# A two-block transformer kernel: tile 0 of the last stage put in order sooner, and its row buffers joined later

## The chip, the cores and the metric

The kernel runs on one core of a Trainium2 chip. A core has five engines with their own instruction queues (TensorE or PE, VectorE or DVE, ScalarE or ACT, GpSimd or POOL, SyncE or SP), which meet only through semaphores, a working memory (SBUF) of 128 partitions, and an accumulator memory (PSUM) of eight banks of 512 floats per partition. Data come from the chip's main memory by DMA. The metric is the time of one execution in microseconds (us); lower is better.

## The reference

One sequence of 256 tokens of width 1024 passes two layers of a first block (gated linear attention beside a state-space mixer, then a dense and an eight-expert feed-forward) and one layer of a second block. The change touches the second block alone:

```python
def token_mixer(h, p, attend):
    z = h @ p['w_in'] + p['b_in']                 # 1024 -> 5120 columns
    q = rmsnorm_2(z[..., COL_Q:COL_K] ...); k = rmsnorm_2(z[..., COL_K:COL_V] ...)
    v = z[..., COL_V:COL_G_HY] ...
    y_hy = hyena(z[..., COL_HY:COL_Q], p) @ p['w_hy_out']     # two long convolutions
    y_na = attend(q, k, v).reshape(B, L, D_NA) @ p['w_na_out']
    gate = jax.nn.sigmoid(z[..., COL_G_HY:N_PROJ])
    merged = gate[..., :D_MODEL] * y_hy + gate[..., D_MODEL:] * y_na
    return merged @ p['w_out']

def peer(h, p):
    q = (hf @ p['peer_w_q']).reshape(T, PEER_HEADS, 2, PEER_D_HALF)     # 8 heads, 2 halves
    s = jnp.einsum('thpd,hpnd->thpn', q, p['peer_keys'])                # 128 keys a half
    top_s, top_i = lax.top_k(s, PEER_TOPK)                              # 16 of each half
    cand_s = top_s[:, :, 0, :, None] + top_s[:, :, 1, None, :]          # 256 sums
    best_s, best_pos = lax.top_k(cand_s, PEER_TOPK)                     # 16 experts
    idx = ...; g = jax.nn.softmax(best_s, axis=-1)
    act = gelu(einsum('td,thkd->thk', xb, u_tab[idx]))                  # 1024 floats a row
    return einsum('thk,thkd->td', g * act, v_tab[idx])                  # 1024 floats a row
...
x_next = x + g1 * token_mixer(modulate(x, ...), p)
x_next = x_next + g2 * peer(modulate(x_next, ...), p)
```

Each token needs 8 x 16 experts, and each expert is one row of 2048 floats (u and v side by side, 8 KB) out of 16384.

## The kernel before, in words

Every engine runs one function, written in the order in which it executes. Where engines meet, the code waits for a semaphore's count. The 256 tokens are two tiles of 128. The work around the change is in three parts.

**The hyena part** (PE L1235 to L1256). Two convolutions `o`, each: turn the input (`ytm`), a transform (`yre`, `yim`), a product on VectorE (`spectrum`), the inverse (`conv`, L684, 128x256 matmuls), and VectorE's update. PE fills its waits with `fill`, which takes the next `piece` of the input projection. A piece (L762) multiplies 256 columns of `w_in`, held in a ring of five 2 MB slots. After it comes the normalising of q, k and kc (L1262 to L1291): PE sums squares (L1269), ScalarE takes the root, VectorE the reciprocal, PE spreads it (L1280), VectorE applies it, PE permutes for the rotary embedding. Between them VectorE works off `hidden`: products of the modulation weights `w_ada` (L1545, four a tile of weights). The gate columns' projections (3072 and 3584, two pieces each) fill PE here. When a slot's last reader is done, SP loads the next weights into it, in its fixed order: `w_hy` into the slot of 3072, then 4096 into that of 3584, then `w_ada`.

**The sixteen head turns** (PE L1366 to L1400; eight heads of tile 0, then eight of tile 1 in `head_turns`, each turn being one head for 128 tokens with i = 0 to 15 and `t` the tile). One turn: VectorE adds the bias and finds the peak (L2037 to L2041), ScalarE exponentiates, VectorE scales (L2047), PE turns the weights (L692) and multiplies by v (L684), in the PSUM banks 4 and 5. Two places in each turn are filled: with `first` (the products of `y_hy` and the last gate pieces) while t = 0, then with `na0` (y_na's product), `out0` (`w_out`, L1340) for tile 0, whose attention is complete after turn 7. Then follow tile 0's residual (`added`), squares, their sum (L1354), a root, a spread (L1361), `normed` and ScalarE's shift, after which tile 0 can ask for experts: `query` (L1422), `key_scores` (L1435), and on VectorE `choices`.

**The row stage** (256 rows, i // 128 the tile, i % 128 = 16 x head + place). POOL issues an indirect DMA for each row: 128 experts, one a partition, 1 MB. VectorE takes the dot product with the tokens (L2199), ScalarE gelu, VectorE multiplies by the gate (L2178), ScalarE makes a diagonal, and PE accumulates 8 matmuls (L1473). Between rows VectorE makes the `choices` of the head after next, PE the remaining queries. `row_places` says which of 16 buffers each row uses. Eight exist at the start; the others are memory that query weights still hold, and join in pairs:

```python
    joins = {50: (8, 9), 82: (10, 11), 98: (12, 13), 116: (14, 15)}
    for i in range(256):
        turn.extendleft(joins.get(i, ()))
        b = turn.popleft()
        turn.append(b)
        ...
                lambda: (at(0), P["pq", 5]),
                lambda: (at(14618), P["pq", 7]),
                lambda: (part(("w_pq", 0), 0), P["pq", 9]),
                lambda: (part(("w_pq", 1), 0), P["pq", 11])
```

Before the first use of such a buffer POOL waits (L2703) for the query that was its last reader: jobs 5, 7, 9 and 11, whose last parts stand in PE's program ahead of rows 44, 76, 93 and 111 (`job_rows`). Any other buffer is free when PE is done with the row it held. POOL's queue is in order: what stands behind a waiting row waits as well.

## Time and profile before

| | us |
|---|---|
| median of 3 runs | 2723.76 (2721.18 to 2724.1) |
| the profiled execution | 2724.18 |
| its span, first to last instruction | 2721.7 |
| PE busy in it | 2522.6 |
| VectorE busy | 2074.8 |
| ScalarE busy | 1256.5 |
| POOL busy | 265.9 |
| bytes moved | 824.92 MB, mean 303 GB/s |

The profile's page gives busy times, a line of 40 slices of 68 us, and the chain of work that ended last. The second block takes roughly the time from 1640 us, the head turns 1877 to 1998, the rows 2020 to 2717. All times below are from the span's start.

### The profile page before, as it was taken

What the parts mean: (1) busy time and instruction counts of PE and PEld (TensorE: products, weight loads), DVE (VectorE), ACT (ScalarE), POOL (GpSimd) and SP (SyncE); (2) the same over time, 40 slices, a digit from 0 to 9 for tenths busy, and PEclk for the clock granted to TensorE, in tenths of its full rate; (3) what the DMA queues carried; (4) which work ended last, traced back from release to release, by engine and by line L of the source; (5) the groups of instructions that cost most, each with busy time, mean ns of one, the idle gap of its engine ahead of it and who ended that gap; (6) DMA issues with size and microseconds to landing.
All of it is one profiled execution on the core that took longest, in us unless ns stands there. A gap on an engine that the chain in (4) does not pass through costs nothing. (4 is left out here: it accounts for less than half of the span.)

```text
span 2721.7 us, 38026 instructions
## 1 busy us (share of the span) xinstructions
PE 2522.6 (93%) x14586; PEld 2183.4 (80%) x14586; DVE 2074.8 (76%) x3114; ACT 1256.5 (46%) x1544; POOL 265.9 (10%) x286
## 2 busy tenths in 40 slices
PE   5999999999999999999999989988988998888787
PEld 4789997787888888888888877647887987787786
DVE  6778984767898989889998964535758785698875
ACT  3234443236777777777777753102323332233322
POOL 0000001000000000000000000000013333343331
PEclk9989999989999999999999998999989999899899
DMA  8647774547999999999999945304749998899997
GB/s 344 248 173 291 277 287 180 230 180 296 355 355 356 356 339 349 356 357 355 354 355 353 356 170 211 124 31 163 286 157 357 391 421 335 368 419 421 420 420 325
DMA packets 109562, 824.92 MB, mean 303 GB/s; under 512 B 11896, under 2 KB 15224, under 8 KB 16128
## 3 DMA queue, kind: packets, MB, share of 16 engines
q1 hardware_dynamic: 71792, 551.75, 53.3%
q0 software_dynamic: 36864, 268.45, 24.1%
q8 instruction: 117, 1.92, 0.3%
q10 hardware_dynamic: 720, 2.24, 0.2%
q14 instruction: 69, 0.57, 0.1%
HBM read 821.34 MB, written 1.05 MB: 302 GB/s over the span
## 5 line engine op out<-in xcount | busy, mean ns | idle before, releaser
L1811 DVE TENSOR_TENSOR ring_r<-ring,arena_r 128x2048 fp32r<-128x2048 f32 x336 | 770.1, 2292 | 11.5
L2225 ACT ACTIVATE arena_r<-ring 128x2048 fp32r<-128x2048 f32 x378 | 725.7, 1920 | 28.9 <-DMA ring<-in_ffn_w_down 12.8
L698 PE MATMUL ps<-arena_r 128*128 128x512 f32 (+1 forms) x1120 | 417.2, 373 | 1.5 <-DVE arena_r L1847 1.5
L700 PE MATMUL ps<-arena_r 128*128 128x512 f32 x896 | 349.3, 390 | 0.0
L699 PE MATMUL ps<-ring_r,arena_r 128*128 128x512 f32 x896 | 348.6, 389 | 0.0
L1473 PE MATMUL ps<-sel,ring 128*128 128x128 f32 x2240 | 291.3, 287 | 58.4 <-ACT sel L2225 45.5
L1473 PEld LDWEIGHTS ps<-sel,ring 128*128 128x128 f32 x2240 | 274.3, 200 | 73.9 <-ACT sel L2225 58.2
L2225 ACT ACTIVATE sel<-cs,arena 128x128 f32<-128x128 f32 x256 | 102.8, 402 | 402.4 <-DVE arena L2178 374.5
L1473 PE MATMUL ps<-sel,arena 128*128 128x128 f32 x1856 | 235.0, 287 | 43.1 <-ACT sel L2225 41.7
L1473 PEld LDWEIGHTS ps<-sel,arena 128*128 128x128 f32 x1856 | 224.8, 201 | 50.5 <-ACT sel L2225 48.5
L2225 ACT ACTIVATE arena<-ps 128x512 f32<-128x512 f32 (+2 forms) x208 | 103.4, 497 | 328.4 <-PE ps L684 94.5
L698 PEld LDWEIGHTS ps<-arena_r 128*128 128x128 f32 x1120 | 211.3, 189 | 35.6 <-DVE arena_r L1847 1.8
L2199 DVE CUSTOM_DVE_ANT_0 accb<-ring,ps 128x1024 f32<-128x1024 f32 x140 | 171.0, 1221 | 52.9 <-DMA ring<-in_uv,arena 49.8
L700 PEld LDWEIGHTS ps<-arena_r 128*128 128x128 f32 x896 | 168.2, 188 | 35.7
L699 PEld LDWEIGHTS ps<-ring_r,arena_r 128*128 128x128 f32 x896 | 168.4, 188 | 34.2
L2704 POOL DMA_INDIRECT ring<-in_uv,arena x140 | 131.9, 942 | 624.8 <-DVE arena L2059 368.0
L699 PE MATMUL ps<-arena_r 128*128 128x256 f32 x672 | 192.5, 286 | 0.0
L698 PE MATMUL ps<-arena_r,h_r 128*128 128x512 f32 x448 | 178.4, 398 | 3.0 <-DVE ring_r L1811 1.7
L700 PE MATMUL ps<-arena_r,h_r 128*128 128x512 f32 x448 | 175.2, 391 | 0.0
L699 PE MATMUL ps<-ring_r,h_r 128*128 128x512 f32 x448 | 174.8, 390 | 0.0
L2225 ACT ACTIVATE arena<-arena 128x1 f32<-128x1 f32 (+5 forms) x361 | 112.6, 312 | 107.8 <-DVE arena L2004 17.3
L2199 DVE CUSTOM_DVE_ANT_0 accb<-arena,ps 128x1024 f32<-128x1024 f32 x116 | 141.6, 1221 | 25.2 <-DMA arena<-in_uv,arena 21.3
(285 smaller groups left out, 3894.3 us busy)
## 6 DMA issues: line engine op xcount, KB each, us to landing
ring<-in_moe_w_gate SPq DMA_DIRECT2D x112, 1024.0 KB, 5.0
ring<-in_moe_w_up SPq DMA_DIRECT2D x112, 1024.0 KB, 5.2
ring<-in_moe_w_down SPq DMA_DIRECT2D x112, 1024.0 KB, 4.9
ring<-in_ada_w SPq DMA_DIRECT2D x24, 1024.0 KB, 9.8
ring<-in_ada_w SPq DMA_DIRECT2D x12, 2048.0 KB, 7.9
ring<-in_w_in SPq DMA_DIRECT2D x10, 2048.0 KB, 12.1
ring<-in_w_ada SPq DMA_DIRECT2D x8, 2048.0 KB, 8.2
ring<-in_ffn_w_gate SPq DMA_DIRECT2D x14, 1024.0 KB, 5.1
```

Of the source, the lines that this page charges most:

```text
L698: e.matmul(out, xs[0], ws[0], start=start, stop=False, skip_group_check=True)
L699: e.matmul(out, xs[0], ws[1], start=False, stop=False, skip_group_check=True)
L700: return e.matmul(out, xs[1], ws[0], start=False, stop=stop, skip_group_check=True)
L1473: last = e.matmul(ps.banks[2 * t + c // 4][:, 128 * (c % 4):128 * (c % 4) + 128], rows[:, 1024 + 128 * c:1152 + 128 * c], m.diag[:, i % ND ...
L1811: v(e.tensor_tensor(ring_low[ring.half[unit]], ring.buf[unit], mo.high[unit_at[unit] % NHIGH].bitcast(F32), ALU.subtract), ("low", unit))
L2199: v(e.tensor_tensor_reduce(m.waste, row_buffer(i)[0][:, 0:1024], x, 1.0, 0.0, ALU.mult, ALU.add, m.dots[:, i:i + 1]), ("dots", i))
L2225: A.mark(e.activation(out, src, func, **kw), name)
L2704: e.indirect_dma_start(base, None, T["uv"], bass.IndirectOffsetOnAxis(m.index[t][:, n:n + 1], 0)).then_inc(row_sems[ROWS[i][0]], 16)
```

## The change

Five edits.

1. `joins` moves from rows 50, 82, 98, 116 to 54, 88, 106, 126.
2. The two pieces of projection 3072 are cut into four halves: two inside the second convolution, two behind it. Their results stay in PSUM banks 0 and 1 (`HELD`), since their place in SBUF is still occupied by the filters, and the second convolution rotates over banks 2 to 7 (`REST`). 3584 takes the fills of q and k; kc has two halves of the `y_hy` product.
3. VectorE does four `hidden` products ahead of the first peak and fewer in the turns; merging moves up one turn.
4. In the turns of tile 1 `na0`, `out0`, the squares, root, spread, norm and shift move one or two turns earlier, and the first query is asked in turn 15.
5. Tile 0's head 0: the best 8 of each half give 64 sums, whose best 8 are the first 8 experts; the second best 8 and all 256 sums follow behind. Squares and sum of tile 1 move two rows up, `exp_gates` of head 1 stands beside the root at row 8 (it was row 8, the root row 7), query job 2 is asked one row sooner, and from the second head on `choices` skips each fourth row.

```diff
-    joins = {50: (8, 9), 82: (10, 11), 98: (12, 13), 116: (14, 15)}
+    joins = {54: (8, 9), 88: (10, 11), 106: (12, 13), 126: (14, 15)}
...
+            gates = chain.from_iterable(piece(3072, i, 2, hT, "hT x", HELD) for i in range(2))
             for o in range(2):
+                among = REST if o else range(8)
...
+                if o:
+                    next(gates)
                 for k in range(2):
...
                 fill(1)
+                if o:
+                    next(gates)
                 e.wait_ge(*V["spectrum", o, 1])
...
             P.at["hyena done"] = P.now
+            next(gates)
+            next(gates)
...
-            pieces = [piece(c0, i, 2, hT, "hT x") for c0 in (3072, 3584) for i in range(2)]
+            pieces = [piece(3584, i, 2, hT, "hT x") for i in range(2)]
...
+                if x == "kc":
+                    next(first)
                 fill(1)
...
-            fill(1)
+            next(first)
...
                 if t == 0:
                     some(first, 1)
-                elif i < 10:
-                    some(na0, 1)
-                elif i < 12:
+                elif i == 8:
+                    some(na0, 2)
+                elif i < 11:
                     some(out0, 2)
+                elif i == 13:
+                    peer_spread(0)
                 elif i == 15:
-                    peer_spread(0)
+                    query(0, 0)
...
-                elif i == 12:
+                elif i == 11:
                     peer_sums(0)
+                elif i == 15:
+                    query(0, 1)
...
+            some(hidden, 4)
             peak(0)
...
                 if i < 8:
-                    some(hidden, 3)
+                    some(hidden, 3 if 3 <= i < 7 else 2)
...
-                if i == 14:
+                if i == 12:
                     rstd(("norm_peer", 0), pr.scr[:, 2048:2049])
-                if i == 15:
+                if i == 13:
                     normed(0, range(8))
...
                 if t == h == 0:
-                    top8(m.cand, m.bs, m.bp)
-                    yield from experts_of(t, h, 0, 8)
+                    for q in range(2):
+                        top8(*places[q])
+                    sums_of(8)
+                    top8(m.cand[:, 0:64], m.bs, m.bp)
+                    yield from experts_of(t, h, 0, 8, 8)
                     for n in range(2):
                         merged_na(1, n)
-                    next8(m.cand, m.bs, m.bp)
+                    for q in range(2):
+                        next8(*places[q])
...
-                if i % 16 == (4 if j else 12):
+                if i % 16 == (4 if j else 9):
...
-                next(later, None)
+                if j == 0 or i % 4 != 3:
+                    next(later, None)
...
-                if i == 14:
+                if i == 12:
+                    root(("norm_peer", 0), ps.bank["norm_peer", 0][:, 0:1], D, pr.scr[:, 2048:2049])
+                if i == 14:
+                    peer_shift(0, range(8))
...
-            peer_shift(0, range(8))
-            table(ACT.Exp)
...
-                if i == 7:
+                if i == 8:
+                    exp_gates(*HEADS[1])
                     root(("norm_peer", 1), ps.bank["norm_peer", 1][:, 0:1], D, pr.scr[:, 2049:2050])
```

On PE, from the second convolution's turned input (L692) to the key norm. `h,ring3` is projection 3072, `h,ring4` is 3584, `arena,ring3` in the second excerpt is `y_hy`'s product. Before:

```order
L692 MATMUL ps<-cs,arena 128x128 x8
L684 MATMUL ps<-arena 128x512 x4
L684 MATMUL ps<-ring2,arena 128x512 x8
L684 MATMUL ps<-pv,cs 128x512
L684 MATMUL ps<-arena 128x512 x4
L684 MATMUL ps<-arena 128x256 x16
L1269 MATMUL ps<-cs,arena 128x2 x8
L762 MATMUL ps<-h,ring3 128x256 x16
L1280 MATMUL ps<-cs,arena 64x128 x16
```

After the change:

```order
L694 MATMUL ps<-cs,arena 128x128 x8
L764 MATMUL ps<-h,ring3 128x256 x8
L686 MATMUL ps<-arena 128x512 x4
L686 MATMUL ps<-ring2,arena 128x512 x8
L686 MATMUL ps<-pv,cs 128x512
L686 MATMUL ps<-arena 128x512 x4
L764 MATMUL ps<-h,ring3 128x256 x8
L686 MATMUL ps<-arena 128x256 x16
L764 MATMUL ps<-h,ring3 128x256 x16
L1280 MATMUL ps<-cs,arena 128x2 x8
L764 MATMUL ps<-h,ring4 128x256 x16
L1293 MATMUL ps<-cs,arena 64x128 x16
```

All of 3072 now stands ahead of the first sum of squares (L1280 now).

On PE, the end of the head turns, from turn 12 on (L1361 is tile 0's spread, L1422 its first query). Before:

```order
L692 MATMUL ps<-cs,arena 128x128 x4
L684 MATMUL ps<-arena 64x128 x4
L1354 MATMUL ps<-cs,arena 128x1 x8
L692 MATMUL ps<-cs,arena 128x128 x4
L684 MATMUL ps<-arena 64x128 x4
L692 MATMUL ps<-cs,arena 128x128 x4
L684 MATMUL ps<-arena 64x128 x4
L692 MATMUL ps<-cs,arena 128x128 x4
L1361 MATMUL ps<-cs,arena 128x128
L684 MATMUL ps<-arena 64x128 x4
L1422 MATMUL ps<-h,ring2 128x128 x16
```

After, from turn 12 on too (the sum stands one turn further up):

```order
L694 MATMUL ps<-cs,arena 128x128 x4
L686 MATMUL ps<-arena 64x128 x4
L694 MATMUL ps<-cs,arena 128x128 x4
L1374 MATMUL ps<-cs,arena 128x128
L686 MATMUL ps<-arena 64x128 x4
L694 MATMUL ps<-cs,arena 128x128 x4
L686 MATMUL ps<-arena 64x128 x4
L694 MATMUL ps<-cs,arena 128x128 x4
L1400 MATMUL ps<-h,ring2 128x128 x8
L686 MATMUL ps<-arena 64x128 x4
L1400 MATMUL ps<-h,ring2 128x128 x8
```

The spread moved from turn 15 to turn 13, and half of the query stands inside turn 15.

On POOL, the issues around the third join; `ring2` is the memory of the first query weights, rows 98 and 99 before. Before:

```order
L2704 DMA ring0<-in_uv,arena 128x2048
L2704 DMA arena<-in_uv,arena 128x2048 x6
L2704 DMA ring4<-in_uv,arena 128x2048
L2704 DMA ring2<-in_uv,arena 128x2048 x2
L2704 DMA ring4<-in_uv,arena 128x2048
```

After, rows 106 and 107:

```order
L2735 DMA ring0<-in_uv,arena 128x2048
L2735 DMA arena<-in_uv,arena 128x2048 x2
L2735 DMA ring4<-in_uv,arena 128x2048
L2735 DMA ring2<-in_uv,arena 128x2048 x2
L2735 DMA ring4<-in_uv,arena 128x2048
```

The pair stands eight rows later in the queue.

## Rows read from the trace of the kernel before

**Rows 1.** Stretches: length, busy of five engines (instructions), PE clock, DMA share, GB/s.
```profile
1877.49:1982.00 104.51, 96.16 (x594) 80.53 (x593) 68.65 (x130) 36.56 (x76) 0.00 (x0) 0.97 0.68 272
...
2020.00:2130.00 110.00, 95.31 (x767) 91.98 (x766) 92.26 (x264) 37.62 (x96) 37.25 (x39) 0.97 0.92 345
2130.00:2160.00 30.00, 26.95 (x214) 25.60 (x213) 25.15 (x72) 10.20 (x27) 10.30 (x11) 1.00 1.01 421
2290.00:2300.00 10.00, 10.00 (x92) 10.00 (x91) 4.73 (x13) 2.20 (x7) 1.88 (x2) 1.00 0.08 16
2340.00:2360.00 20.00, 19.24 (x169) 18.81 (x168) 12.16 (x35) 5.01 (x16) 6.63 (x8) 1.00 0.60 242
...
2164.60:2672.80 508.20, 429.81 (x3338) 410.75 (x3337) 386.18 (x1038) 156.59 (x438) 190.16 (x203) 0.93 0.97 401
2470.20:2672.80 202.60, 166.10 (x1288) 156.70 (x1288) 153.91 (x407) 62.25 (x175) 75.54 (x81) 0.94 1.01 420
```

**Rows 2.** POOL's waits from 2160 to 2360: total us, times, longest.
```profile
POOL ring L2704 <- PE ps L1422: 45.3, 2, 24.2
...
POOL arena L2704 <- PE ps L1422: 14.7, 2, 10.3
```

**Rows 3.** POOL in order of time, the third and fourth join: start, length, idle before.
```profile
2297.66 0.94 POOL L2704 DMA_INDIRECT ring<-in_uv,arena  x1 [21.11 <-PE ps L1422]
...
2351.24 0.94 POOL L2704 DMA_INDIRECT ring<-in_uv,arena  x1 [24.23 <-PE ps L1422]
```

**Rows 4.** PE in order of time, second convolution to the first scores.
```profile
1819.72 8.74 PE L684 MATMUL ps<-arena 128*128 128x256 f32 x32 [4.48 <-DVE arena L1998]
1830.83 1.92 PE L1269 MATMUL ps<-cs,arena 128*128 128x2 f32 x16 [2.37 <-ACT arena L2225]
...
1870.38 7.17 PE L762 MATMUL ps<-h,ring 128*128 128x256 f32 x32
1877.49 2.00 PE L1302 MATMUL ps<-arena 64*128 64x256 f32 x16
```

**Rows 5.** VectorE in order of time, the first peak and the first `hidden` product of the turns.
```profile
1879.23 0.42 DVE L2037 SCALAR_TENSOR_TENSOR arena<-ps,ring 128x256 f32<-128x256 f32 x1 [7.92 <-ACT arena L2225]
...
1891.42 1.29 DVE L1545 CUSTOM_DVE_ANT_0 sel<-ring,accb,pv 128x1024 f32<-128x1024 f32 x1 [1.49 <-DMA ring<-in_w_ada]
```

**Rows 6.** SP's DMA issues in order of time: the weight tiles of the head turns.
```profile
1877.96 0.91 SPq L543 DMA_DIRECT2D ring<-in_w_ada  x2
```

**Rows 7.** PE in order of time, turn 12 and the first query.
```profile
1982.00 0.60 PE L692 MATMUL ps<-cs,arena 128*128 128x128 f32 x4
...
2001.69 6.45 PE L1422 MATMUL ps<-h,ring 128*128 128x128 f32 x32 [3.94 <-issue]
```

**Rows 8.** ScalarE in order of time: tile 0's root and shift.
```profile
1992.51 1.28 ACT L2225 ACT_TABLE_LOAD   x1
1993.80 0.26 ACT L2225 ACTIVATE arena<-ps,small 128x1 f32<-128x1 f32 x1
...
1998.16 3.44 ACT L2225 ACTIVATE h<-h,mods 128x128 f32<-128x128 f32 x8
```

**Rows 9.** VectorE in order of time: head 0's choice, its first index, the first dot product.
```profile
2010.96 0.29 DVE L2113 MAX8 arena<-arena 128x8 f32<-128x128 f32 x1 [11.76 <-ACT arena L2225]
...
2011.69 0.09 DVE L2117 MATCH_VALUE_LOAD arena<-arena 128x8 f32 x1
...
2019.09 0.17 DVE L2136 SCALAR_TENSOR_TENSOR arena<-arena 128x8 int32<-128x8 f32 x1
...
2026.99 1.22 DVE L2199 CUSTOM_DVE_ANT_0 accb<-ring,ps 128x1024 f32<-128x1024 f32 x1
```

**Rows 10.** VectorE: a stalled coefficient before row 9; the dot product of row 48.
```profile
2059.13 0.16 DVE L2178 TENSOR_TENSOR arena<-arena 128x1 f32<-128x1 f32 x1 [2.42 <-ACT arena L2225]
...
2164.60 1.22 DVE L2199 CUSTOM_DVE_ANT_0 accb<-ring,ps 128x1024 f32<-128x1024 f32 x1
```

**Rows 11.** The chain of waits that ended last, one step near its end: start, length.
```profile
2477.45 33.38 DMA ring<-in_uv,arena
```

More of the change, by code:

```diff
@@ L167 @@
 ASIDE = (2, 3, 6, 7)
+HELD = (0, 1)
+REST = (2, 3, 4, 5, 6, 7)
 NROWS = 16
@@ L1251, in pe @@
                     s = slice(128 * c, 128 * c + 128)
-                    b = bank(("conv", o, c))
+                    b = bank(("conv", o, c), among)
                     P.mark(summed(b[:, 0:256], [(m.yre[:, k, s], m.DCI[:, k, :]) for k in range(2)]
@@ L1256, in pe @@
             P.at["hyena done"] = P.now
+            next(gates)
+            next(gates)
             e.wait_ge(*V["hyena done"])
             e.wait_ge(*A["hyena done"])
-            pieces = [piece(c0, i, 2, hT, "hT x") for c0 in (3072, 3584) for i in range(2)]
-            behind_heads = [branch("w_hy", m.zc, i // 2, i % 2, ASIDE[2:]) for i in range(4)]
-            behind_heads += [piece(c0, i, 2, hT, "hT x", ASIDE[2:]) for c0 in (4096, 4608) for i in range(2)]
+            pieces = [piece(3584, i, 2, hT, "hT x") for i in range(2)]
+            pieces_later = [branch("w_hy", m.zc, i // 2, i % 2, ASIDE[2:]) for i in range(4)]
+            pieces_later += [piece(c0, i, 2, hT, "hT x", ASIDE[2:]) for c0 in (4096, 4608) for i in range(2)]
+            first = chain.from_iterable(pieces_later)
             for x in ("q", "k", "kc"):
@@ L1367, in some, with query @@
                     next(pieces, None)
-            first = chain.from_iterable(behind_heads)
+            def query(j, n):
+                h, ts = JOBS[j]
+                tile = v4(pq_tile(h // 2), 8)
+                if n == 0:
+                    if h < 4:
+                        arrived(("w_pq", h // 2))
+                    else:
+                        e.wait_ge(*(in_pq2 if h < 6 else in_pq3))
+                    if j == 4:
+                        e.wait_ge(*A["hT peer", 1, 7])
+                    bank(("pq", j), (2, 3))
+                q, ks = (n, range(8)) if len(ts) == 1 else (n // 2, range(4 * (n % 2), 4 * (n % 2) + 4))
+                c, x = 256 * (h % 2) + 128 * q, slice(128 * ts[0], 128 * ts[-1] + 128)
+                out = ps.bank["pq", j][:, 128 * len(ts) * q:128 * len(ts) * (q + 1)]
+                for k in ks:
+                    if j == n == 0:
+                        e.wait_ge(*A["hT peer", 0, k])
+                    last = e.matmul(out, tile[:, k, c:c + 128], hT[:, k, x], start=(k == 0), stop=(k == 7))
+                if q and k == 7:
+                    P.mark(last, ("pq", j))
             na0, out0 = na(0), out2(0)
@@ L1404, in pe @@
             na1, out1 = na(1), out2(1)
-            def query(j, n):
-                h, ts = JOBS[j]
-                tile = v4(pq_tile(h // 2), 8)
-                if n == 0:
-                    if h < 4:
-                        arrived(("w_pq", h // 2))
-                    else:
-                        e.wait_ge(*(in_pq2 if h < 6 else in_pq3))
-                    if j in (0, 4):
-                        e.wait_ge(*A["hT peer", ts[-1], 7])
-                    bank(("pq", j), (2, 3))
-                q, ks = (n, range(8)) if len(ts) == 1 else (n // 2, range(4 * (n % 2), 4 * (n % 2) + 4))
-                c, x = 256 * (h % 2) + 128 * q, slice(128 * ts[0], 128 * ts[-1] + 128)
-                out = ps.bank["pq", j][:, 128 * len(ts) * q:128 * len(ts) * (q + 1)]
-                for k in ks:
-                    last = e.matmul(out, tile[:, k, c:c + 128], hT[:, k, x], start=(k == 0), stop=(k == 7))
-                if q and k == 7:
-                    P.mark(last, ("pq", j))
             def key_scores(j):
@@ L1444, in pe @@
             keys = ring.buf["keys"]
-            for n in range(2):
-                query(0, n)
             some(na1, 1)
@@ L2553, in act @@
                 fill()
-            fill()
             def context_score(i):
```

84 lines of the change are left out of this document (45 added, 39 removed).

## The prediction

> **What bounds the kernel now.** I read the stretches first, then POOL's waits, then the engines' time lines back from the row stage to the second convolution. The change begins at 1797 us, so only the last 920 us matter.
>
> The chain of waits near its end is DMA: a gather takes 33.4 us from issue to landing, because 16 stand in the queue [rows 11]. From 2470.2 to 2672.8 the core moves 420 GB/s and the DMA engines are busy throughout, while VectorE works 153.9 and PE 166.1 of 202.6 us [rows 1]. Those are the 80 rows 160 to 239, 2.53 us each, which is the pace of DMA. Over rows 48 to 239 the mean is only 401 GB/s in 508.2 us. The same bytes at 420 take 508.2 x 401 / 420 = 485.2 us, so 23.0 us of DMA time are lost there. By the rows: 192 x 2.5325 = 486.2, so 22.0.
>
> Where they are lost is plain: 2290 to 2300 has 16 GB/s, 2340 to 2360 has 242 [rows 1]. POOL waited in that region four times for the last query in PE's order (L1422), 60.0 us together [rows 2], the two longest 21.1 and 24.2 us, at rows 98 and 116 [rows 3]. Those are the first rows of the third and fourth join. Row 98 with ten buffers needs only row 88's buffer to go on, but takes the new one, which waits for job 9, asked before row 93; row 116 waits for row 111's query and would have needed row 104 (with 12 buffers). Meanwhile DMA runs out of requests. So the row stage is bound by DMA wherever it is fed, and by POOL's in-order queue at the joins.
>
> Before row 48 it is otherwise: 345 GB/s with VectorE busy 92.3 of 110 us [rows 1]. There it follows VectorE, PE and the chain that leads to the first gather.
>
> **Joins.** New firsts: row 54 with 8 buffers in use follows the release of row 45, and its own needs the query ahead of row 44; row 88 (10 buffers) follows row 77, needs 76; row 106 (12) follows 93, needs 93; row 126 (14) follows 111, needs 111. In each case the predecessor in POOL's queue has already waited for PE to reach that point, so the wait is nothing new. What it costs is depth: 4, 6, 8 and 10 rows run with two buffers fewer. From 2130 to 2160, with eight buffers, DMA moved 421 GB/s [rows 1], so eight are enough there, and more so 10, 12, 14. PE was busy 26.95 and VectorE 25.15 of those 30 us, so both keep that pace, PE with little to spare. Gain: 22 us. Bounds: 12, if rows that VectorE or PE handle late leave dips with the shallower queue, and 23.
>
> A rule speaks against this. The Trainium skill ("DMA: Bandwidth & Descriptors", Bandwidth) says that for transfers between main memory and SBUF the memory side binds, at about 358 GB/s a core. By that rule the mean of 401 would already lie above the limit and filling the holes would give nothing. The row of 80 gathers at 420 contradicts it here [rows 1], so the sum goes by 420.
>
> **Second convolution and key norm.** A half of a piece is 7.17 / 2 = 3.6 us [rows 4]. The first stands where PE waits for VectorE's two copies anyway; of its 3.6 us I count 2.4 as delay of the transform. The second stands in the idle of 4.48 us before the inverse [rows 4], at no cost, and as PE then idles less, the inverse should take some 7.2 instead of 8.74. It ends at about 1829 instead of 1828.5. Then two halves, 7.2 us, lie in front of q's sum, which starts at 1836.4 instead of 1830.8. ScalarE and VectorE are served 5.6 us later, of which the next fill gives back 1.5 (8.8 became 7.2). So kc's part begins 4.1 us late, but there PE has 2 + 2 us of `y_hy` instead of two pieces of 7.2. kc is then bound by VectorE's rotation of k: first scores at about 1871.8 instead of 1877.5 [rows 4]: 5.7 sooner, with 4 us of later filling done.
>
> VectorE's four products take 4 x (1.29 and a short read) = 5.3 us and lie in its idle of 7.92 us before the first peak [rows 5]. They need a weight tile. It landed at 1891.4 before [rows 5], because SP issued it at 1878.0, behind the load that waits for 3584's last reader [rows 6]. That reader ends at about 1859 now (in k's fill), so the tile lands at 1859.6 + 13.4 = 1873.0, just when VectorE is free of kc. First peak at 1878.3 instead of 1879.2. So 5.7 us of head start on PE become about 1.3 us for the first turn.
>
> **Head turns.** PE is nearly saturated from the first scores at 1877.5 to the end of tile 0's `w_out` product at 1982.0 [rows 4, 7]: 96.2 of 104.5 us busy [rows 1], 8.4 idle. Now 4.0 of its work are done before and turn 11's 2.8 come behind: 89.4 us of work. Idle grows: 5.6 before turn 0 (VectorE), 4 around turns 0 to 2, where a bank of `y_hy` must be merged first, 2.5 before turn 8, 3 elsewhere, 15 in all. 1871.8 + 89.4 + 15 = 1976.3: 5.7 us sooner.
>
> **Tile 0's chain.** From there to the end of the first query it was 2008.1 - 1982.0 = 26.1 us: four turns, then a root late at 1993.8, the spread after turn 15, shift 3.44, query 6.45 [rows 7, 8]. Now root, norm and shift lie in turns 12 to 14, but five turns of 4.3 us remain, VectorE's norm (3.0) stands before turn 15's scaling, and ScalarE's shift before its copy. Step by step I come to 26.5: the chain is no longer behind the turns, it is among them. Taken: 0.4 lost. Bounds: 4 sooner, 3 later. One cost is new: the root's table comes before the exponential of turn 14, so a load of 1.28 us stands in a turn. The next activation starts 0.01 us after such a load [rows 8].
>
> The Trainium skill ("ScalarE: Activation LUTs", What ACT_TABLE_LOAD costs) counts 2.66 us a switch, the load plus a drain. By it the turn would lose 1.4 us more. The trace shows no drain here, so 1.28 stands.
>
> **First experts.** From ScalarE's scores to the first index it was 2019.26 - 2010.96 = 8.3 us [rows 9]. Twice the second best 8 (2 x 1.1), a fourth of the sums, and half as wide comparisons fall away: about 5.1, so 3.2 us sooner. That helps rows 0 to 2 only. Row 3 waits for PE's `w_out` product of tile 1, which comes 5.3 us sooner with the chain. In front of the first dot product VectorE has 0.7 us more in all, so it starts 5.3 - 0.7 = 4.6 sooner than 2027.0 [rows 9].
>
> **Rows 0 to 47.** VectorE waits some 2.3 us a row for ScalarE's gelu at rows 7 to 10 [rows 10], which stands behind four table loads and a query. One load goes (1.28 us), and head 2's choice starts at row 9 in that idle. I take 1 us: row 48 comes 4.6 + 1.0 = 5.6 us sooner than 2164.6 [rows 10]. Bounds for everything up to row 48: 1 and 11.
>
> **Sum.** 5.6 + 22.0 = 27.6 us. The profiled execution took 2724.2 (span 2721.7 and 2.5 around it): 2696.6. The runs' median is 0.4 lower: **2696 us**.
>
> **Rivals.**
> - *Half of the joins' gain.* PE and VectorE have only 10 and 16% to spare in the stretch with eight buffers [rows 1], and the shallower queue drains in the rows with a choice. Joins give 11: 2707. For it, rows 1; against it, no dip from 2130 to 2160.
> - *Nothing in front.* The 5.7 us of `w_out` are eaten in the turns of tile 1, where the norm and shift sit in VectorE's and ScalarE's way; the joins give 22: 2702. For it, five turns instead of four.
> - *The joins still wait.* If a buffer's last reader came after the row I counted, or the memory side bound as the skill's rule has it, only the front's 5.6 remain: 2718. Against it, the four rows are the queries' own and 420 GB/s were reached.
> - *Slower.* Two buffers fewer in 28 rows bring DMA to the 345 GB/s of the early rows [rows 1]: 3.04 us a row, 28 x 0.5 = 14 us; joins give nothing, and the weight tile lands as late as before, so that the first peak starts at 1896.7, 17.5 late, of which PE's advance hides 10. 14 + 7 - 6 = 15 us: 2739. It decides if eight gathers in the queue do not fill DMA; rows 1 say they do.
>
> **Numbers.** Forecast 0.66, half of the joins 0.14, nothing in front 0.12, joins still wait 0.04, slower 0.04. Its own range is 2688 to 2703; with the two next rivals the range is 2687 to 2710, which leaves out about 0.15. A change of under 0.2% (5.4 us) can't be told from none: faster means below 2718.3. Faster 0.93, same 0.03, slower 0.04.
>
> **What would show it.** Right: no wait of POOL for L1422 (now L1400) over 5 us; no stretch of 10 us under 380 GB/s between rows 48 and 239, which take 486 us; first scores near 1872, tile 0's `w_out` product done near 1976, first query near 2003, first gather issued near 2011.5, first dot product near 2022.4. Wrong: a hole at rows 50 to 130 as before; the first peak behind 1885; a first query later than 2006. The forecast fails first if the depth of the queue, and not POOL's wait, makes the holes.

## The result, and the profile after

| | before | after |
|---|---|---|
| median | 2723.27 us (4 runs) | 2690.22 us (4 runs, 2688.51 to 2693.61) |
| the profiled execution | 2724.18, span 2721.7 | 2693.61, span 2691.3 |

The ratio is 0.9882 [0.9867, 0.9898]: 33.1 us less. Forecast were 27.6 us less, 2696 in a range of 2687 to 2710. The time lies in the range; the forecast was 5.8 us too slow, and the sum behind it had one term nearly right and one of half the size. The profiled execution of the changed kernel is the slowest of its four, 3.4 us above their median, so the profiles show 30.6 us of the gain.

**The rows.** Stretches of the changed kernel, columns as in [rows 1]: rows 0 to about 38, the 30 us behind, the two stretches with the holes of before, rows 48 to 239, rows 160 to 239.

```profile
2017.20:2130.00 112.80, 100.66 (x790) 97.73 (x790) 91.40 (x259) 36.48 (x98) 37.63 (x41) 0.94 0.90 346
2130.00:2160.00 30.00, 26.14 (x205) 24.60 (x204) 25.94 (x72) 11.16 (x30) 10.99 (x12) 1.00 1.02 421
2290.00:2300.00 10.00, 9.51 (x86) 9.32 (x84) 7.94 (x23) 2.44 (x8) 3.72 (x4) 1.00 1.01 422
2340.00:2360.00 20.00, 15.68 (x136) 15.10 (x135) 17.75 (x48) 7.87 (x21) 7.10 (x8) 1.00 1.01 420
2155.47:2642.45 486.98, 405.38 (x3337) 386.04 (x3336) 386.78 (x1038) 156.67 (x438) 189.46 (x202) 1.00 1.01 420
2439.80:2642.45 202.65, 157.76 (x1282) 147.31 (x1281) 153.98 (x407) 62.28 (x175) 75.35 (x81) 1.00 1.01 420
```

The holes of 16 and 242 GB/s [rows 1] are gone; rows 48 to 239 run at 420 GB/s in 487.0 us instead of 508.2. The last 80 rows take 202.65 us as they did 202.60, so their pace was DMA's before and is now. POOL's waits from 2160 to 2360 (total us, times, longest) name the queries no more, where [rows 2] had 60.0 us:

```profile
POOL ring L2735 <- PE ps L1489: 55.8, 31, 2.7
POOL arena L2735 <- PE ps L1489: 42.6, 29, 3.5
```

L1489 is PE's sum over the row that held the buffer. The longest wait is 3.5 us and starves nothing.

**The front.** The profiled executions differ by up to 5 us before the change begins (the turned input of the second convolution comes at 1797.69 before and 1797.53 after, at 1792.7 to 1795.3 in the experiments). Below, times of different kernels are therefore counted from that input ("from the input"). PE in order of time, inverse of the second convolution to the first scores (L1315), against [rows 4]:

```profile
1821.54 7.17 PE L686 MATMUL ps<-arena 128*128 128x256 f32 x32 [1.03 <-DVE arena L2014]
1828.56 7.07 PE L764 MATMUL ps<-h,ring 128*128 128x256 f32 x32
1835.46 1.84 PE L1280 MATMUL ps<-cs,arena 128*128 128x2 f32 x16
...
1868.80 1.99 PE L686 MATMUL ps<-arena,ring 128*128 128x256 f32 x8
1870.72 2.00 PE L1315 MATMUL ps<-arena 64*128 64x256 f32 x16
```

The wait of 4.48 us before the inverse is 1.03, and the first scores come 6.8 us sooner. SP issues the next weight tile 20 us sooner than in [rows 6] (first fence), and VectorE uses it before the first peak (second fence), not after it as in [rows 5]:

```profile
1858.28 0.91 SPq L545 DMA_DIRECT2D ring<-in_w_ada  x2
```

```profile
1870.37 1.28 DVE L1561 CUSTOM_DVE_ANT_0 sel<-ring,accb,pv 128x1024 f32<-128x1024 f32 x1 [0.64 <-DMA ring<-in_w_ada]
...
1875.69 0.42 DVE L2053 SCALAR_TENSOR_TENSOR arena<-ps,ring 128x256 f32<-128x256 f32 x1
```

PE from the end of tile 0's `w_out` product to the first query (L1400). The turn that follows this product was turn 12 in [rows 7], at 1982.00; with edit 4 it is turn 11:

```profile
1973.72 0.60 PE L694 MATMUL ps<-cs,arena 128*128 128x128 f32 x4
...
1991.25 1.12 PE L694 MATMUL ps<-cs,arena 128*128 128x128 f32 x4
1992.16 2.56 PE L1400 MATMUL ps<-h,ring 128*128 128x128 f32 x16
1994.65 1.09 PE L686 MATMUL ps<-arena 128*64 128x128 f32 x8
1995.67 2.05 PE L1400 MATMUL ps<-h,ring 128*128 128x128 f32 x16
1997.56 1.95 PE L686 MATMUL ps<-arena 128*128 128x128 f32 x16
```

The query is done at 1997.6 instead of 2008.0 (taken at the start of the product behind it). Its first half starts when ScalarE is 2.9 us into the shift, not behind it:

```profile
1989.27 3.44 ACT L2254 ACTIVATE h<-h,mods 128x128 f32<-128x128 f32 x8
```

VectorE in order of time, against [rows 9] and [rows 10]: head 0's choice, its first index, the first dot product, and row 48's:

```profile
2000.54 0.29 DVE L2131 MAX8 arena<-arena 128x8 f32<-128x128 f32 x1 [9.45 <-ACT arena L2254]
...
2005.43 0.17 DVE L2155 SCALAR_TENSOR_TENSOR arena<-arena 128x8 int32<-128x8 f32 x1
...
2017.20 1.22 DVE L2227 CUSTOM_DVE_ANT_0 accb<-ring,ps 128x1024 f32<-128x1024 f32 x1
```

Index to first dot product is 11.8 us, before it was 7.9: VectorE has put its work off, not away. Row 48's dot product starts at 2155.47, 9.1 us sooner than before.

So 21.2 us of the profiled gain lie in rows 48 to 239 and 9.1 ahead of them.

### The profile page after: what moved, and what is told of

Read it like the earlier page. It is cut to its first block, busy times and chain, and to the rows that moved or that the text cites. A ratio compares the mean times of both kernels' runs of the same rounds, so it can differ in the third digit from the quotient of the medians.

```text
span 2691.3 us, 38029 instructions
## 1 busy us (share of the span) xinstructions
PE 2496.1 (93%) x14586; PEld 2159.8 (80%) x14586; DVE 2076.1 (77%) x3119; ACT 1255.4 (47%) x1542; POOL 266.2 (10%) x286
## 4 chain that ended last, share of the span: by engine, by line
PE 73%; DMA 13%; DVE 7%; issue 4%; ACT 1%; POOL 0%; SPq 0%; DVEq 0%; ACTq 0%; another core or an unknown queue 0%; POOLq 0%
PE ps L700 14%; PE ps L702 14%; PE ps L701 14%; DMA ring<-in_uv,arena 10%; PE ps L686 7%; PE ps L764 5%; PE ps L1489 4%; PE ps L719 4%; DMA arena<-in_uv,arena 3%; PE ps L694 2%; PE ps L1353 1%; PE ps L924 1%; PE ps L936 1%; PE ps L1400 1%; PE ps L1081 1%
## 5 line engine op out<-in xcount | busy, mean ns | idle before, releaser
L1489 PE MATMUL ps<-sel,ring 128*128 128x128 f32 x2272 | 280.6, 280 | 61.2 <-ACT sel L2254 59.2
L1489 PEld LDWEIGHTS ps<-sel,ring 128*128 128x128 f32 x2272 | 265.1, 193 | 74.0 <-ACT sel L2254 70.6
L1489 PE MATMUL ps<-sel,arena 128*128 128x128 f32 x1824 | 230.0, 282 | 44.4 <-ACT sel L2254 43.4
L1489 PEld LDWEIGHTS ps<-sel,arena 128*128 128x128 f32 x1824 | 215.8, 195 | 55.6 <-ACT sel L2254 55.2
```

What stands on the lines that cost most here:

```text
L1489: last = e.matmul(ps.banks[2 * t + c // 4][:, 128 * (c % 4):128 * (c % 4) + 128], rows[:, 1024 + 128 * c:1152 + 128 * c], m.diag[:, i % ND ...
```

## The experiments

Twelve kernels. The first four ran on one chip, the next four on a second, the last four on a third. On the third the kernel before took 2710.93 us, 12 less than on the others, while experiments 11 and 12, which ran there, took what the changed kernel took elsewhere. I have no trace of the kernel before from there and can't say why. Each experiment ran on one chip only, and the changed kernel was not run again beside them; so "more than the changed kernel" compares two chips, and differences under some 2 us say nothing.

**1. The joins alone, in the kernel before.**

```diff
-    joins = {50: (8, 9), 82: (10, 11), 98: (12, 13), 116: (14, 15)}
+    joins = {54: (8, 9), 88: (10, 11), 106: (12, 13), 126: (14, 15)}
```

> The kernel before with the one line of joins changed to 54, 88, 106, 126. Theory A (POOL's wait at a joined row lets DMA run dry): the four waits for L1422 (60.0 us together before) shrink to under 5 us each, rows 48 to 239 take 486 to 488 us instead of 508.2, nothing before row 48 moves by more than 1 us, and the time is 2723.3 - 21.5 = 2702. Theory B (the holes come from too shallow a queue, or from PE and VectorE, and the changed kernel filled them through its other edits): the time stays at 2720 or above, with dips under 380 GB/s left between rows 48 and 128.

Measured: 2702.61 us (2700.67 to 2704.44), 0.9930 [0.9913, 0.9947]: 20.6 us less. The stretch with the holes, 2130 to 2340:

```profile
2130.00:2340.00 210.00, 192.31 (x1602) 186.28 (x1601) 169.06 (x461) 71.53 (x199) 83.60 (x90) 1.00 1.01 420
```

POOL's longest wait there is 3.5 us, and none is for the query. Rows 48 to 239 take 487.1 us instead of 508.2. The joins are worth 20.6 on this chip, and the wait for the query was the cause.

**2. The old joins in the changed kernel** (the same diff, reversed).

> The changed kernel with the old joins 50, 82, 98, 116. Theory A: everything up to row 48 is as in the changed kernel (first gather near 2006.5, row 48 near 2155.5), rows 48 to 239 take 508 us again, so 2690.2 + 21.5 = 2711.7. Theory B: the other edits keep the queue fed, and it stays within 5 us of 2690.

Measured: 2708.33 (2706.32 to 2711.0), 0.9951 [0.9935, 0.9968]: 18.1 more than the changed kernel. Rows 48 to 239 take 506.0 us. The holes are back in the same stretch, and the two longest waits of POOL (last fence, columns as in [rows 3]) are near the 21.1 and 24.2 us of [rows 3]:

```profile
2130.00:2340.00 210.00, 186.72 (x1476) 178.21 (x1475) 154.84 (x419) 67.33 (x185) 71.42 (x76) 0.97 0.92 376
```

```profile
2279.54 0.94 POOL L2735 DMA_INDIRECT ring<-in_uv,arena  x1 [19.33 <-PE ps L1400]
...
2334.30 0.94 POOL L2735 DMA_INDIRECT ring<-in_uv,arena  x1 [26.09 <-PE ps L1400]
```

**3. Eight buffers to the end.**

```diff
-    joins = {54: (8, 9), 88: (10, 11), 106: (12, 13), 126: (14, 15)}
+    joins = {}
```

> The changed kernel with no joins at all: eight row buffers to the end, POOL never waits for a query. Theory A (eight gathers in the queue are enough for DMA): rows 48 to 239 take 486 to 492 us, the time is 2690 to 2697. Theory B (the depth of the queue matters): DMA falls to the 345 to 380 GB/s of the early rows, 2.8 to 3.0 us a row for the 170 rows after the second join, 50 to 80 us longer, 2740 or more.

Measured: 2691.22 (2689.33 to 2692.15), 0.9885 [0.9869, 0.9902], the same as the changed kernel. Rows 48 to 239 take 488.5 us at 416 GB/s, against 487.0 at 420, with single stretches of 10 us down to 365 GB/s. Eight gathers of 1 MB keep DMA nearly full; the eight buffers that join are worth 1.5 us in the trace and nothing that the times could show. The rival of a shallow queue falls.

**4. Head 2's choice from row 12 again.**

```diff
-                if i % 16 == (4 if j else 9):
+                if i % 16 == (4 if j else 12):
```

> The changed kernel with head 2's choice begun at row 12 as before, not at row 9. In the changed kernel row 48's dot product comes 9.1 us sooner than before though the first comes 9.8 sooner, so rows 0 to 47 gained nothing, and DMA moves only 279 and 226 GB/s from 2060 to 2080. Theory C (the choice begun at row 9 fills VectorE when rows 9 to 15 should go through, and holds buffers back): without it row 48 comes 2 to 4 us sooner, 2687. Theory D (VectorE has the same work up to row 48 wherever it stands): within 1.5 us of 2690.

Measured: 2689.58 (2687.85 to 2691.24), 0.9879 [0.9863, 0.9896]. No difference. Row 16 came 2.7 us sooner from the input than in the changed kernel (276.8 against 279.6), row 48 only 1.1. Neither is an effect of the edit that I could tell: experiment 2, with the changed kernel's code up to there, has row 16 at 276.4, experiment 3 at 280.4.

**5. No 64 sums.** Head 0 again makes all 256 sums before its first index.

```diff
-                    for q in range(2):
-                        top8(*places[q])
-                    sums_of(8)
-                    top8(m.cand[:, 0:64], m.bs, m.bp)
-                    yield from experts_of(t, h, 0, 8, 8)
+                    top8(m.cand, m.bs, m.bp)
+                    yield from experts_of(t, h, 0, 8)
```

> The changed kernel with head 0 chosen as before, from all 256 sums. Counted from the second convolution's start (c2; the first gather stands at c2 + 209.0 in the changed kernel and c2 + 222.5 before). Theory E (row 3 and the rest wait for PE's w_out product, so sooner rows 0 to 2 are worth nothing): the first gather comes 3 us later, c2 + 212, the first dot product within 1 us, row 48 within 1 us of c2 + 358, the time within 1.5 us of 2690. Theory F (the first gathers fill an empty DMA and everything follows): row 48 and the time 3 us later, 2693.

Measured: 2689.67 (2688.12 to 2690.37), 0.9880 [0.9863, 0.9896], the same. From the input the first gather comes at 212.9 instead of 209.0 (209.7 in experiments 3 and 4), the first dot product at 219.8 against 219.7. From ScalarE's scores to the first index it is 8.3 us, and 5.1 with the 64 sums. They bring the first gather 3.2 us forward and nothing behind it: the first dot product stands behind VectorE's own work, which is the same in sum.

**6. Projection 3072 back in the key norm**, with VectorE's four products still ahead of the first peak.

```diff
-            pieces = [piece(3584, i, 2, hT, "hT x") for i in range(2)]
+            pieces = [piece(c0, i, 2, hT, "hT x") for c0 in (3072, 3584) for i in range(2)]
...
```

> The changed kernel with projection 3072 back among the key norm's fills (edit 2 undone), while VectorE still does four hidden products ahead of the first peak. Theory G (SP can issue the weight tile only behind 3584's last reader): the tile lands near c2 + 94, the first peak stands near c2 + 99 instead of c2 + 79, turn 0 near c2 + 103 instead of c2 + 83. PE has less filled in than before, so most of it stays: row 48 10 to 18 us later, 2700 to 2708. Rival H (the turns catch up, since PE's fills can go ahead and VectorE has less to do afterwards): 2691 to 2696.

Measured: 2707.25 (2706.82 to 2707.89), 0.9945 [0.9928, 0.9961]: 17.0 more than the changed kernel. SP issues the weight tile at 1877.89, and VectorE, which would have the first peak to do, stands before it:

```profile
1889.88 1.28 DVE L1552 CUSTOM_DVE_ANT_0 sel<-ring,accb,pv 128x1024 f32<-128x1024 f32 x1 [18.64 <-DMA ring<-in_w_ada]
```

Edit 3 is only bearable with edit 2. This is the mechanism of my prediction's slower rival, forced: its condition (a late tile) did not hold in the changed kernel. The late peak was sized about right: 17.5 us after the peak of the kernel before were forecast, and it comes 100.0 us from the input here against 81.5 there. The price in time is not tested by it. The rival let PE's advance hide 10 of the 17.5; here PE has no advance (first scores 82.2 us from the input, 79.8 before), and 17.0 us are lost against the changed kernel.

**7. Edits 2 and 3 both undone**: as 6, and besides

```diff
-            some(hidden, 4)
             peak(0)
...
-                if i < 4:
-                    merged_hy(i)
+                if 1 <= i < 5:
+                    merged_hy(i - 1)
...
-                    some(hidden, 3 if 3 <= i < 7 else 2)
+                    some(hidden, 3)
```

> The changed kernel with edits 2 and 3 undone (3072 in the key norm, three hidden products a turn, merging as before); tile 0's chain and the rest as changed. Expected from the forecast's steps: first scores at c2 + 80 again instead of c2 + 73 to 75, the end of tile 0's w_out product 4 to 6 us later than c2 + 176, row 48 3 to 6 us later, 2694 to 2696. Rival: it brings nothing because the turns are bound by VectorE's products either way, within 1.5 us of 2690.

Measured: 2694.61 (2693.9 to 2695.8), 0.9900 [0.9884, 0.9917]: 4.4 more than the changed kernel. Tile 0's `w_out` product ends 182.3 us from the input instead of 176.2, row 48's dot product at 362.2 instead of 357.9. Of 6.1 us on PE 4.4 reach the end.

**8. Tile 0's chain in its old order** (edit 4 undone; the first query kept its chunk-wise wait, see 9).

```diff
-                if i == 12:
+                if i == 14:
                     rstd(("norm_peer", 0), pr.scr[:, 2048:2049])
-                if i == 13:
+                if i == 15:
                     normed(0, range(8))
...
+            for n in range(2):
+                query(0, n)
             some(na1, 1)
```

> The changed kernel with edit 4 undone (na0, out0, squares, root, spread, norm, shift and first query where they stood). The forecast gave this edit 2.8 - 0.4 = 2.4 us; the trace of the changed kernel says that the end of the w_out product to the end of the query took 23.9 us instead of 26.1, so 2.8 + 2.2 = 5 us. If the trace is read rightly the first gather stands near c2 + 214 and the time is 2694 to 2696; if the forecast's 2.4 was right, c2 + 211.4 and 2692.5. With e7 it should make up the 9.0 us that row 48 gained over before.

Measured: 2690.44 (2689.37 to 2692.13), 0.9885 [0.9869, 0.9902]: the same as the changed kernel, a miss of my expectation. The query ends 201.1 us from the input, against 200.0 in the changed kernel and 200.8 in experiments 3 and 4, which have its code up to there. PE, turn 15's product and the query:

```profile
1987.35 1.24 PE L686 MATMUL ps<-arena 128*64 128x128 f32 x8 [0.32 <-ACT arena L2251]
1989.54 5.22 PE L1400 MATMUL ps<-h,ring 128*128 128x128 f32 x32 [0.95 <-DVE h L2091]
```

Where [rows 7] had the query 3.94 us idle behind turn 15, and 6.45 us long, it is 0.95 and 5.22 here, with the same order of turns. The new thing is not the order but a line that I had passed over in the diff.

**9. The same, with the query's wait as before.** That line, taken back in experiment 8's kernel:

```diff
-                    if j == 4:
-                        e.wait_ge(*A["hT peer", 1, 7])
+                    if j in (0, 4):
+                        e.wait_ge(*A["hT peer", ts[-1], 7])
...
                 for k in ks:
-                    if j == n == 0:
-                        e.wait_ge(*A["hT peer", 0, k])
```

> The changed kernel with tile 0's chain as before, this time also with the first query waiting for the whole of tile 0's shift instead of one of its eight chunks at a time. With the chain in the old order but the chunk-wise wait, the time was 2690.4, the same as the changed kernel, and from turn 12 to the end of the first query it took 21.9 us, against 26.3 with the old chain and the old wait (the kernel before with the new joins). Theory H (what edit 4 is worth is the chunk-wise wait, which my prediction left out): first query ends 4.4 us later against turn 12, first dot product 4 us later, 2694 to 2695. Rival I (a sooner first query is worth nothing, since VectorE's work and the banks set the early rows): 2690 to 2691.

Measured: 2695.55 (2692.59 to 2696.84), 5.1 more than experiment 8 and 5.7 more than experiment 12 from the same chip. The row of before is back:

```profile
1988.99 1.25 PE L686 MATMUL ps<-arena 128*64 128x128 f32 x8 [0.32 <-ACT arena L2249]
1994.18 6.39 PE L1398 MATMUL ps<-h,ring 128*128 128x128 f32 x32 [3.94 <-issue]
```

"Issue" as the releaser hid it: PE stood at a semaphore for the last chunk of the shift, and the row does not say so.

The 4.2 us between the two kernels (25.9 from turn 12 to the query's end here, 21.8 in experiment 8) are more than overlap. Stretches with the columns of [rows 1], the query of this kernel up to its 25th record, then the whole query of experiment 8:

```profile
1994.18:1999.44 5.26, 5.26 (x25) 5.26 (x25) 0.00 (x0) 1.41 (x2) 0.00 (x0) 0.50 0.95 403
```

```profile
1989.54:1994.76 5.22, 5.22 (x34) 4.33 (x35) 0.60 (x2) 4.18 (x9) 0.00 (x0) 1.00 1.02 377
```

Behind 3.94 us of idle PE had the lower clock, 0.50 (1.2 GHz), for 25 of the 32 records that the query's 16 matmuls have in the profile; they start 0.21 us apart, the last seven 0.11 apart. Behind 0.95 us of idle it had 1.00 throughout. The same pair is in the other traces: 0.57 over the query before and 0.56 in experiment 1, both behind 3.94 us of idle, 1.00 in experiments 10 and 12 behind 0.95. At the upper clock the query would have taken some 2.5 us less here (25 x 0.10, an estimate from these starts), so of the 4.2 us about 2.5 are the clock and 1.7 the overlap.

**10. That line alone**, in the kernel before with the new joins.

```diff
-                    if j in (0, 4):
+                    if j == 4:
                         e.wait_ge(*A["hT peer", ts[-1], 7])
...
                 for k in ks:
+                    if j == n == 0:
+                        e.wait_ge(*A["hT peer", 0, k])
```

> The kernel before with the new joins and one line more: the first query waits for each of the eight chunks of the shift instead of for the last. The kernel before with the joins alone took 2702.6. Theory H: PE begins the query during the shift, 3.9 us of its idle time go, the first gather and first dot product come 4 us sooner, 2698 to 2699. Rival I: the query ends sooner but the end does not move, 2702 to 2703.

Measured: 2697.08 (2696.43 to 2698.72), 5.5 less than the joins alone (2702.61, on another chip; the pair from one chip, 9 and 12, gives 5.7, with the 64 sums besides, which were worth nothing in 5). From turn 12 to the query's end 21.9 us instead of 26.3, row 48's dot product 4.7 us sooner from the input.

```profile
1997.84 5.22 PE L1424 MATMUL ps<-h,ring 128*128 128x128 f32 x32 [0.95 <-DVE h L2079]
```

**11. The first rows in their old order.**

```diff
-                if i == 3:
+                if i == 5:
                     peer_sums(1)
...
-                if i == 8:
-                    exp_gates(*HEADS[1])
+                if i == 7:
                     root(("norm_peer", 1), ps.bank["norm_peer", 1][:, 0:1], D, pr.scr[:, 2049:2050])
```

and likewise `added(1)`, the squares, job 2, the start of head 2's choice and the skipped rows.

> The changed kernel with the order of the first rows as before: tile 1's squares and sum two rows later, root at row 7 apart from the exponential at row 8, second query job one row later, choices of head 2 from row 12, no skipped rows. Theory J (the early rows are bound by VectorE and its waits for ScalarE behind table loads, and this order removes one of four loads): VectorE's stalls at rows 7 to 10 grow by 2 to 4 us, row 48's dot product comes 2 to 3 us later, 2692 to 2694. Rival K (DMA takes over near row 20 and swallows such differences, as it did with the choice moved from row 9 to 12): 2690 to 2691.

Measured: 2690.79 (2689.48 to 2691.93). VectorE's three stalls of 2 us are back, as [rows 10] had them, in place of the changed kernel's 1.51, 3.70 and 1.00:

```profile
2041.82 0.16 DVE L2206 TENSOR_TENSOR arena<-arena 128x1 f32<-128x1 f32 x1 [2.19 <-ACT arena L2253]
...
2045.66 0.16 DVE L2206 TENSOR_TENSOR arena<-arena 128x1 f32<-128x1 f32 x1 [2.42 <-ACT arena L2253]
...
2049.46 0.16 DVE L2206 TENSOR_TENSOR arena<-arena 128x1 f32<-128x1 f32 x1 [1.97 <-ACT arena L2253]
```

Yet row 48 comes at 358.1 us from the input, against 357.9. My expectation of 2 to 3 us more falls; that order is worth nothing.

**12. The 64 sums and the moves of the chain undone together**, the chunk-wise wait kept (the diffs of 5 and 8).

> The changed kernel with two edits undone together that were worth nothing when undone one at a time: the 64 sums, and the moves of tile 0's chain into earlier turns (the chunk-wise wait stays). Theory L (each is worth nothing by itself because VectorE's work between the first index and the first dot product is the same in sum, so the two add up to nothing too): first gather 5 us later than in the changed kernel, first dot product 1 us, 2690 to 2692. Rival M (each covers for the other: with both gone the first rows lack their data): first dot product 4 to 5 us later, 2694 to 2695.

Measured: 2689.90 (2688.26 to 2690.91), the same as the changed kernel. The two don't cover for each other: together too they are worth nothing.

All in one table, from the input of the second convolution, in us (medians in the last column). The first column is the end of tile 0's `w_out` product; turn 12 follows it in the kernels with the old chain (before, 1, 10, 9, 8, 12), turn 11 in 7 and after:

| kernel | w_out end | query's end | first gather | first dot | row 48 | rows 48-239 | time |
|---|---|---|---|---|---|---|---|
| before | 184.3 | 210.3 | 222.5 | 229.3 | 366.9 | 508.2 | 2723.3 |
| 1 joins alone | 185.6 | 211.9 | 224.1 | 231.0 | 368.9 | 487.1 | 2702.6 |
| 10 and chunk-wise wait | 185.7 | 207.6 | 219.8 | 226.6 | 364.2 | 487.9 | 2697.1 |
| 9 edit 4 all undone | 179.4 | 205.3 | 214.2 | 224.9 | 362.2 | 488.1 | 2695.6 |
| 7 edits 2, 3 undone | 182.3 | 205.7 | 214.6 | 225.3 | 362.2 | 487.8 | 2694.6 |
| 8 edit 4's moves undone | 179.4 | 201.1 | 210.1 | 220.7 | 356.7 | 487.9 | 2690.4 |
| 12 and no 64 sums | 176.9 | 198.8 | 211.0 | 217.8 | 354.3 | 488.3 | 2689.9 |
| after | 176.2 | 200.0 | 209.0 | 219.7 | 357.9 | 487.0 | 2690.2 |

A single profile of one kernel is worth some 1 to 3 us here: 8 and 12 do the same work up to turn 12 and differ by 2.5, and the changed kernel and experiment 2 (173.6) by 2.6. In both pairs the slower one has the lower granted clock from the input to there, 0.96 against 0.98. So the first column's 179.4 against 176.2 is not a gain of the moves: one turn (2.8 us by my forecast) went from ahead of this mark to behind it.

## Why the prediction was right, and where it was not

**The bound** was right. Rows 48 to 239 take 487.0 us (486 forecast) at DMA's pace; no stretch of 10 us in them is below 380 GB/s and no wait of POOL for a query is left. The Trainium skill ("DMA: Bandwidth & Descriptors", Bandwidth) has the memory side bind at about 358 GB/s a core. The same section gives that figure as a core's share when its neighbour streams too, and 425 GB/s measured for one core alone. This program runs on one core, and its 420 over 487 us agrees with the second figure; the rule that my prediction set against itself was not the one for this case.

**Joins**: 22.0 us forecast, 20.6 measured (experiment 1), 18.1 when taken back from the changed kernel (experiment 2). My bounds were 12 and 23. The cost in depth that I set at nothing is at most 1.5 us with eight buffers to the end (experiment 3). One reading of the old order was off: at row 98 twelve buffers were in use and the next free one was row 86's, at row 116 fourteen and row 102's (not ten and 88, twelve and 104). The argument gains by it, since the old buffers were free still sooner.

**The front**: 5.6 us forecast, 12.4 measured (2702.61 - 2690.22, medians from two chips). This is the term that was mis-sized, and 12.4 is above its upper bound of 11. At row 48 the traces give 9.0 against the kernel before and 11.0 against experiment 1. That the sum still fell in the range is owed to the width of the range. The first dot product came 5.2 us before the forecast time, 2.6 of them up to the end of tile 0's `w_out` product and 2.7 in the chain behind it. By its parts:

- *Key norm and first peak.* First scores 5.7 us sooner forecast, 6.8 measured; of the idle of 4.48 us before the inverse a half piece was to fill 3.6, and 1.03 is left; inverse 7.2 us, measured 7.17. The weight tile was to land at 1873.0 and did before 1870.4; the first peak was to start at 1878.3 and started at 1875.7. (1878.3 is 0.9 us before the 1879.2 of [rows 5], and not the 1.3 that the prediction goes on with.)
- *Head turns.* From the first scores to turn 12 I had 89.4 us of work and 15 idle; they were 90.75 and 12.25:

```profile
1870.72:1973.72 103.00, 90.75 (x558) 77.54 (x557) 66.08 (x125) 33.53 (x69) 0.00 (x0) 0.93 0.58 228
```

  The `w_out` product ended at 1973.7 instead of the 1976.3 forecast; 2.6 us is also what same code differs by with the clock (176.2 and 173.6 from the input). With edits 2 and 3 undone the time rises by 4.4 us (experiment 7).
- *Tile 0's chain: the step that failed.* "Step by step I come to 26.5 ... Taken: 0.4 lost." From the end of the `w_out` product to the query's end it took 23.8 us. The four turns 11 to 14 took 17.5 (4 x 4.3 = 17.2 forecast). Turn 15 with the query took 6.3, where the forecast leaves 9.3. The steps are not written out, but the only length named for the query is the 6.45 us of [rows 7], a row with granted clock 0.57 behind 3.94 us of idle. Inside turn 15, with no idle ahead of it, the two halves took 2.56 and 2.05: 1.8 us less, at a clock of 0.83 over the turn. It also had VectorE's norm of 3.0 hold up turn 15, which yet began 3.8 us after turn 14.

```profile
1991.25:1997.56 6.31, 6.31 (x45) 6.02 (x45) 0.00 (x0) 2.24 (x6) 0.00 (x0) 0.83 0.19 42
```

- *The line that the prediction passed over.* In the old order of the chain the chunk-wise wait is worth 5 us of time (experiments 9 and 10). In the changed kernel's order it can't be worth that: there the first half of the query starts at 1992.16, and ScalarE's shift is done at 1992.71, so waiting for the whole shift would cost some 0.6 us (an estimate from these two rows). The moves and the line are two ways to one gain: neither 2695.6, the line alone 2690.4, both 2690.2. The moves without the line were not run. So "the moves are worth nothing" is shown only beside the line, and whether they would bring the 5 us by themselves is open.
- *First experts.* "3.2 us sooner" is what was measured, scores to first index (8.3 and 5.1 us), and "helps rows 0 to 2 only" holds. I still let 0.7 us of added work count, and took the rest of the gain from elsewhere; the measured worth is nothing (experiment 5).
- *Rows 0 to 47*: 1.0 us forecast. From the first dot product to row 48 it was 137.6 us before and 138.3 after: 0.7 lost. Undoing that part of edit 5 changes nothing (experiment 11).
- *Table loads.* The two in the turns were 1.28 us each, at 1979.91 and 1981.70, one more than I had named. They cost PE little: turn 13 took 4.95 us from its first product to that of turn 14, and 4.54 in experiment 8, which has neither the loads nor the spread there:

```profile
1979.91 1.28 ACT L2254 ACT_TABLE_LOAD   x1
1981.20 0.26 ACT L2254 ACTIVATE arena<-ps,small 128x1 f32<-128x1 f32 x1
1981.70 1.28 ACT L2254 ACT_TABLE_LOAD   x1 [0.23 <-DVE arena L2057]
1982.99 0.72 ACT L2254 ACTIVATE arena<-arena 128x512 f32<-128x512 f32 x1
```

  The Trainium skill ("ScalarE: Activation LUTs", What ACT_TABLE_LOAD costs) would count 2.66 us with a drain; here the next activation starts 0.01 us after each load, so no drain is seen.

**The rivals.** Half of the joins' gain, and joins that still wait, fall with experiment 1. "Nothing in front" was right for the 64 sums and the row order, and for the moves as long as the chunk-wise wait is there; it was wrong for edits 2 and 3 and for the wait it did not know of. The slower rival's mechanism exists (experiment 6), its condition did not hold.

**What adds up.** 2723.3 less 20.6 (joins), 5.5 (chunk-wise wait, experiment 10) and 4.4 (edits 2 and 3, experiment 7) is 2692.8, 2.6 above 2690.2. The edits are not independent, and their order matters. Where the chain is old, edits 2 and 3 with the row order bring 7.2 us (experiment 10 to 12, on one chip). Where edits 2 and 3 are missing, the moves with the 64 sums and the row order bring 2.5 us (experiment 10 to 7, whose times don't overlap: 2696.4 to 2698.7 and 2693.9 to 2695.8, on two chips); where they stand, nothing. Why early gains fade is not shown. In the changed kernel DMA moves 226 to 384 GB/s in the stretches of 10 us from 2030 to 2100 and 418 to 424 in each from 2100 to 2660; the dot product of row 25 stands at 2098. That DMA takes over near row 25 and sets the rest fits the small differences at row 48, but one profile differs from the next by as much. No kernel here was faster than the changed one by more than its spread; experiments 3 and 12 reach its time with less.

## What to carry to other kernels

In an in-order queue, a new buffer that waits for a late reader blocks all the old ones behind it: let it join when its reader is done anyway, and ask first whether it is needed (here eight buffers did as well as sixteen). Where a consumer waits for the last piece of a producer that works in pieces, wait piece by piece; this one change of a wait was worth 5 us in the old order, and the moves of the chain nothing beside it. Before calling an edit worthless because undoing it costs nothing, ask whether another covers for it. And when you take an instruction's length from a row, look at the granted clock in that row and at the idle ahead of it: some 2.5 of the query's 6.45 us were slow clock. Read a diff for its waits as carefully as for its order, and when a step brings an issue forward, see what the same engine has put behind it: the 64 sums brought the first gather 3.2 us forward and the first dot product not at all.

## What the runs showed of the hardware

- One core read 420 GB/s of 8 KB rows over 487 us with up to sixteen gathers of 1 MB in the queue, and 416 GB/s with eight (488.5 us for the same rows).
- Thirty-two matmul records of the query took 6.4 to 6.6 us behind 3.94 us of idle (granted clock 0.56 to 0.58, before and in experiments 1 and 9) and 5.2 behind 0.95 (1.00, in 8, 10 and 12).
- PE's granted clock over rows 160 to 239 was 0.94 before [rows 1] and 1.00 after, its busy time 166.1 and 157.8 us, and the stretch took 202.60 and 202.65 us: a slower PE is free where DMA sets the pace.
- The kernel before took 2723.2 and 2722.2 us on two chips and 2710.9 (2709.0 to 2714.2) on a third, where experiments 11 and 12 took what the changed kernel took elsewhere (2690.8 and 2689.9). So the size of the gain depends on the chip: joins and chunk-wise wait together (experiment 10) bring 13.9 us there, and 26.2 by the time of the kernel before elsewhere. What differs is open.
